# Two-layer decoder trunk on one core: sigmoid and head root moved ahead of four copies, one weighing moved ahead of the conv products, another between them, and fewer filler matmuls at the start

## The reference, cut to what matters

```python
mod = cond @ w_ada[l] + b_ada[l]                       # 1024 -> 6 * 1024
sh1, sc1, gt1, sh2, sc2, gt2 = split(mod, 6)
u = x * (1 + sc1) + sh1
q, k, v, o, i_pre, f_pre, cb, cc, ch = split(u @ w_in[l])
h = mlstm_chunkwise(q, k, v, i_pre, f_pre)             # 4 heads
h = head_norm(h, mh_norm_w[l]) * sigmoid(o)
y_conv = cb * depthwise_conv3(cc * ch)                 # 512 channels
mix = concat([h, y_conv]) @ w_out[l]
x = layer_norm(ALPHA * x + (1 + gt1) * mix)
u = x * (1 + sc2) + sh2
y = hier_moe(u)                                        # 16 experts, 1024 -> 512 -> 1024
x = layer_norm(ALPHA * x + (1 + gt2) * y)
```

## Time and profile before

| what | value |
|---|---|
| undisturbed runs | 839.2 and 839.71 us (a third run read 1674.44; 839.71 is the median of the three) |
| profiled execution: its time, its span | 841.6 us, 839.8 us |
| busy TensorE, VectorE, ScalarE, GpSimd | 94%, 46%, 12%, 9% of the span |
| mean granted clock of TensorE | 0.975 |
| mean traffic | 348 GB/s over the span, 292.54 MB |
| stages: head, mixer 0, routing, experts 0 | 0 to 28, to 184, to 204, to 430 us |
| mixer 1, routing, experts 1, last norm | to 588, to 604, to 828, to 840 us |

### The profile page before, as it was taken

How to read it: one execution, slowest core, us unless ns; L and a number is a source line. 1 busy time by engine, 2 the same in 40 slices (tenths; PEclk the granted TensorE clock), 3 DMA queues, 4 the chain that set the end, 5 groups by cost and what they waited for, 6 DMA issues and landing times.

```text
span 839.8 us, 9226 instructions
## 1 busy us (share of the span) xinstructions
PE 791.5 (94%) x3804; PEld 428.8 (51%) x3823; DVE 390.3 (46%) x818; ACT 98.9 (12%) x213; POOL 71.4 (9%) x94
## 2 busy tenths in 40 slices
PE   7999996989999999999979999699899999999994
PEld 2775685655444344434337658575544434443431
DVE  0138836997433313431346656393643431334135
ACT  2021101103111011101120200110311101110100
POOL 4000150120100000000002303003010000000000
PEclk9999997999999999999989999899999999999998
DMA  9993998797999999999996577487599999999991
GB/s 318 398 403 141 376 373 312 271 401 282 393 407 415 415 409 415 416 409 414 415 409 247 221 297 264 159 308 292 204 393 386 414 413 410 414 416 409 415 413 68
DMA packets 71029, 292.54 MB, mean 348 GB/s; under 512 B 4496, under 2 KB 4776, under 8 KB 62792
## 3 DMA queue, kind: packets, MB, share of 16 engines
q1 hardware_dynamic: 68712, 291.62, 87.9%
q0 software_dynamic: 1216, 0.25, 0.2%
q10 hardware_dynamic: 1056, 0.03, 0.1%
HBM read 290.84 MB, written 1.05 MB: 348 GB/s over the span
## 4 chain that ended last, share of the span: by engine, by line
PE 79%; DVE 9%; DMA 6%; issue 4%; ACT 1%; POOL 1%; DVEq 0%; POOLq 0%
PE bank L806 22%; PE bank L701 13%; PE bank L830 12%; PE bank L793 8%; PE bank L718 7%; DMA ring<-in_w_up_dram 6%; PE bank L852 4%; PE bank L965 2%; DVE bench L1246 2%; PE bank L732 2%; PE bank L577 2%; DVE expo L1246 1%; PE bank L591 1%; PE bank L814 1%; PE bank L860 1%
## 5 line engine op out<-in xcount | busy, mean ns | idle before, releaser
L701 PE MATMUL bank<-uT,ring 128*128 128x256 f32 x512 | 113.4, 381 | 0.0
L701 PEld LDWEIGHTS bank<-uT,ring 128*128 128x128 f32 x512 | 96.4, 190 | 17.0 <-issue 4.3
L830 PE MATMUL bank<-ring,hb 128*64 128x512 f32 x448 | 99.6, 595 | 1.4 <-ACT hb L1103 1.4
L806 PE MATMUL bank<-ring,uT 128*64 128x512 f32 x448 | 99.2, 593 | 1.0 <-DMA ring<-in_w_up_dram 1.0
L806 PE MATMUL bank<-ring,qT 128*64 128x512 f32 x448 | 99.4, 594 | 0.0
L1246 DVE SCALAR_TENSOR_TENSOR bench<-ring,cond,bench 128x1024 f32<-128x1024 f32 x63 | 82.7, 1314 | 4.7 <-DMA ring<-in_w_ada_dram 2.6
L793 PEld LDWEIGHTS bank<-ccT,X 128*128 128x128 f32 x512 | 61.5, 197 | 11.0 <-issue 11.0
L1469 DVE SCALAR_TENSOR_TENSOR kT<-bank,share,v_flat 128x512 f32<-128x512 f32 x32 | 23.9, 748 | 92.3 <-PE bank L830 92.3
L793 PE MATMUL bank<-ccT,X 128*128 128x128 f32 x512 | 64.3, 284 | 0.3 <-DVE ccT L1422 0.3
L806 PEld LDWEIGHTS bank<-ring,uT 128*64 128x64 f32 x448 | 31.6, 137 | 63.7 <-issue 60.5
L830 PEld LDWEIGHTS bank<-ring,hb 128*64 128x64 f32 x448 | 30.9, 137 | 62.8 <-issue 60.5
(11 more groups left out here) (284 smaller groups left out, 704.6 us busy)
## 6 DMA issues: line engine op xcount, KB each, us to landing
ring<-in_w_gate_dram SPq DMA_DIRECT2D x28, 2048.0 KB, 17.2
ring<-in_w_up_dram SPq DMA_DIRECT2D x28, 2048.0 KB, 17.7
ring<-in_w_down_dram SPq DMA_DIRECT2D x28, 2048.0 KB, 15.7
ring<-in_w_ada_dram SPq DMA_DIRECT2D x23, 2048.0 KB, 12.5
ring<-in_w_in_dram SPq DMA_DIRECT2D x14, 2048.0 KB, 16.0
ring<-in_w_out_dram SPq DMA_DIRECT2D x4, 2048.0 KB, 10.3
bench<-in_w_gate_dram SPq DMA_DIRECT2D x4, 2048.0 KB, 13.4
bench<-in_w_up_dram SPq DMA_DIRECT2D x4, 2048.0 KB, 17.3
```

Source lines behind the costliest of these rows:

```text
L701: last = pe.matmul(bank[4 + i // 2][:, i % 2 * SEQ:(i % 2 + 1) * SEQ], w[:, j, col:col + P], uT[:, 4 * k + j, :], start=(k == 0 and j == 0 ...
L806: last = pe.matmul(bank[bk][CAP * j:CAP * (j + 1), :], xg[b][:, 4 * h + k, CAP * j:CAP * (j + 1)], ring[s[h]][:, 4 * j + k, :], start=(h = ...
L830: last = pe.matmul(bank[6 + half][CAP * j:CAP * (j + 1), :], hhT[:, f, CAP * j:CAP * (j + 1)], ring[s[h]][:, 4 * j + 2 * i + half, :], sta ...
```

## The change

It has four parts.

- ScalarE, both layers: the sigmoid and the head root stand ahead of the four `ccT` copies.
- VectorE, both layers: `ada_weigh(l, 9)` stands ahead of the four products, not between the second and the third. In layer 0, two halves of `ada_weigh(1, 1)` stand behind the first and the second product, and no longer ahead of `first_norm`.
- The unit `("ada", 1, 1)` stands ahead of `("proj", 0, 6)` in the list of transfers, four places earlier.
- TensorE: eleven filler matmuls fewer in the head, and three more in each layer ahead of the transposes behind the output projection.

```diff
-               ("proj", 0, 5), ("ada", 0, 8), ("ada", 0, 9), ("proj", 0, 6), ("ada", 0, 10), ("ada", 0, 11), ("wout", 0, 0),
-               ("ada", 1, 1), ("ada", 1, 2), ("ada", 1, 3), ("wout", 0, 1)],
+               ("proj", 0, 5), ("ada", 0, 8), ("ada", 0, 9), ("ada", 1, 1), ("proj", 0, 6), ("ada", 0, 10), ("ada", 0, 11), ("wout", 0, 0),
+               ("ada", 1, 2), ("ada", 1, 3), ("wout", 0, 1)],
...
                 ada_unit(0)
                 stay_busy(3, 3)
                 head_columns(0)
-                stay_busy(6, 3)
+                stay_busy(4, 3)
                 ada_unit(1)
                 small_columns()
-                stay_busy(3, 3)
                 head_columns(1)
                 transpose_x()
-                stay_busy(8, 4)
+                stay_busy(2, 4)
                 pe.wait_ge(uT_act, 4)
...
+                stay_busy(3, 4)
                 transpose_half(0, [(x_ready, 2 * T * l + 1)] * 2, rows_of, by_half)
...
-                for q in range(CH):
-                    act.wait_ge(proj_done, NBLK * l + 14 + 2 * q)
-                    act.activation(ccT[:, q, :], bank[4 + q][:, 0:SEQ], ACT.Copy).then_inc(proj_act, 1)
                 act.wait_ge(proj_act, 16 * l + 12)
                 link(act.activation(o_sig[:, :, :], o_sig[:, :, :], ACT.Ln, bias=1.0))
                 act.activation(o_sig[:, :, :], o_sig[:, :, :], ACT.Exp, scale=-1.0).then_inc(sigmoid_ready, 1)
                 rsqrt(0, T * HEADS, hvar_ready, l + 1, hrs_ready)
+                for q in range(CH):
+                    act.wait_ge(proj_done, NBLK * l + 14 + 2 * q)
+                    act.activation(ccT[:, q, :], bank[4 + q][:, 0:SEQ], ACT.Copy).then_inc(proj_act, 1)
...
+                ada_weigh(l, 9)
                 for q in range(CH):
                     dve.wait_ge(proj_done, NBLK * l + 14 + 2 * q)
                     dve.wait_ge(proj_act, 16 * l + 13 + q)
                     dve.tensor_tensor(zT[:, q, 2:2 + SEQ], ccT[:, q, :], bank[4 + q][:, SEQ:2 * SEQ], ALU.mult).then_inc(proj_dve, 1)
-                    if q == 1:
-                        ada_weigh(l, 9)
+                    if l == 0 and q < 2:
+                        ada_weigh(1, 1, 2 * q, 2 * q + 2)
...
                 if l == 0:
-                    for i in range(1, 4):
+                    for i in range(2, 4):
                         ada_weigh(1, i)
```

## The result

The changed kernel took 812.29 us (median of four runs, 811.26 to 815.0) beside 839.46 for the kernel before: ratio 0.9685, 95% interval [0.9654, 0.9715]. The profiled execution of after took 811.93 us with a span of 810.2; that of before had a span of 839.8. The medians differ by 27.2 us, the two profiled spans by 29.6.

A forecast was written before the change was run, and what follows sets the result against it. TensorE, busy 94%, was taken as the bound, with gains in its waits and half-clock stretches. Layer 0 10.4 + layer 1 9.3 + tail 4.4 + head 2.1 = 26.2 us: 841.6 to 815.4 profiled, median 813.5, range 809.5 to 821.

The forecast's parts named there:

- The wait and the slow stretch: TensorE before the first block: 7.5 us wait goes in each layer, plus slow matmuls of 2.9 and 1.8 us.
- with it goes the stretch at half clock: Layer 0, 48 matmul records behind the wait return to full clock: 13.35 to 10.4, 2.9 us saved.
- VectorE's walk in layer 0: VectorE's new order from ready heads at 116.2 through the products, ending between 127.9 and 132, in time for TensorE.
- GpSimd's share: Layer 0: GpSimd's reductions running beside VectorE's weighing were allowed to add 1 to 4 us.
- The tail: End of layer 0's mixer: VectorE begins the norm earlier, last transposes 3.3 us behind the projection instead of 7.7; 4.4 us.
- The head: Kernel start: eleven fillers removed save 2.6 us, first products at half speed give back 0.5; 2.1 us net.
- 2.6 gross: Kernel start: the eleven removed fillers, at 0.21 to 0.27 us each, save 2.6 us before any clock loss.
- Rival 1: The weight transfer stream caps layer 0, time 822 us; chance 0.15 wholly or in part (816 to 823).
- My walk: Layer 0 transfers: twelve units from 129.5 end at 192.7, just before TensorE's first expert buffer release at 193.3.
- Rivals 2 and 4: Head clock stays low through first products, 816 us, chance 0.12; or far longer, 844 at 60 us, slower, chance 0.02.
- rival 2: Clock stays low under the head's first products, losing 2.9 us, not 0.5; 816 us, chance 0.12.

The follow-up runs named there:

- e12: The changed kernel run and profiled once more, nothing altered: 813.54 us, ratio 0.9672 to the kernel before.
- e1: The kernel before with only ScalarE's sigmoid and head root moved ahead of the four cc copies: 822.16 us, ratio 0.9781.
- e3: The kernel before with 34 filler matmuls inside TensorE's wait ahead of the first block, both layers: 841.78 us, ratio 0.9997.
- e4: The changed kernel with the early unit back in its old place, in the transfer list and on VectorE: 819.38 us, ratio 0.9757.
- e6: The changed kernel without the three fillers ahead of the transposes behind the output projection: 813.28 us, ratio 0.9649.
- e5: The changed kernel with the head's eleven fillers put back: 814.18 us, ratio 0.9656.
- e7: The changed kernel with the tenth unit's weighing back between the second and third product, both layers: 813.04 us, ratio 0.964.
- e11: The kernel before with ScalarE's order, VectorE's order and the early unit's move, but all fillers as before: 814.31 us, ratio 0.9687.
- e8: The kernel before, unchanged, profiled once more: 841.0 us (one run).
- e2: The changed kernel with ScalarE's order of before (copies first), the rest of the change kept: 843.18 us, ratio 1.0023.
- e9: The changed kernel with 32 matmuls left out of layer 0's mixer and two early units weighed with half their operations: 810.04 us, ratio 0.9624.
- e10: The changed kernel with 32 matmuls left out of layer 1's mixer: 808.36 us, ratio 0.9611.

## Why the prediction was right, point by point

The forecast was 813.5 us; 812.29 was measured, and 813.54 in e12. For the profiled execution I forecast 815.4 and got 811.93.

**The wait and the slow stretch, both layers (19.7 forecast).** Right in mechanism and size: 7.5 + 2.8 and 7.5 + 1.7 in the traces, 19.4 by e1 (14 to 23 by its interval). I put the wait down to ScalarE's place in its queue, and e1 moves that alone. The step "with it goes the stretch at half clock" holds in both kernels' rows; e3 shows a condition that I didn't state: in layer 0 the 2.8 us count only if VectorE comes to the norm sooner as well. ScalarE's order sees to that by itself, by 10.7 us in e1.

**VectorE's walk in layer 0.** Forecast: last product done between 127.9 and 132, in the times of before; it was 127.5, and after runs 3.9 us ahead of before there (97.81 for 101.68 at the start of cc/ch), so 131.4, near the end of the range. GpSimd's share: I allowed 1 to 4 us; four operations beside its reduction of 112.70 to 116.77 took 7.10 us, two beside the next 4.13, for 5.2 and 2.60 undisturbed, so 3.4 in all. That is most of the 4.3 us by which the group of 63 is longer (1383 ns for 1314). The Trainium skill ("GPSIMD Engine Reference", 1. Specifications) says that GpSimd shares its SBUF interfaces with VectorE and contends with instructions that have two SBUF inputs, as a weighing has; the trace agrees, by these 3.4 us.

**The tail (4.4 forecast).** 4.7 in the trace, 3.0 us for 7.7. By e4 the early unit's move is worth about 6 in the median; its profile has 4.2 of that in the tail (7.2 for 3.0). The rest is not placed. The three new fillers, which I put at no cost and no gain, keep the clock up there, for 0.8 us (e6).

**The head (2.1 forecast).** 2.2 between the two profiles, but both had a fall of the clock there. At full clock it is 1.7, in three profiles against three, and by medians 0.9 and 1.1 (e5 against e6 and e7), within the noise of each; e11 against e12 gives 0.8 with the tail's fillers in it. The term of "2.6 gross" left out the transfer: 0.69 us of wait take its place.

**Rival 1, the stream of transfers.** It did not bind. My walk had its end at 192.7 and the release at 193.3; they were near 188.7 and 188.71, 4.0 and 4.6 us sooner, since I counted the units from 129.5 with 2 us to start, and the queue had issued the first w_out unit at 126.04 already; the release was sooner by the head, which I had not counted there, by the fall near 74 and by small terms. The margin was as thin as forecast.

**Rivals 2 and 4, the clock in the head.** It was back at 27 as forecast; in e12 it never fell. The Trainium skill's rule on transposes ("TensorE: Matmul & The Clock Gate", Part 4: PE-mode transpose), which I weighed for rival 2, is borne out in part only: the 16 transposes of x took 3.27 us with the clock falling in one profile of before and 1.94 at 1.00 in the other (e8), with the same instructions around them.

**What I left out.** The profile of before carried 12 us of falls of the clock, of which 4.4 belong to the waits. One of the others, near 74, does not come in every execution of the same kernel (before has it and e8 not, e12 has it and after not), and I subtracted my sum from a profile that held it: 1.7 of the 3.5 us between 815.4 and 811.93. The rest are small terms that I had at nothing: 0.3 in the routing, 0.4 at the end, the overlap of records at the two waits, and 0.6 in the experts and projections, which is a difference of falls of the clock. By the medians, which average over the falls, 26.2 was forecast and 27.2 found. That it came so close is in part luck: by medians the head gave about 1 for 2.1 and the early unit some 6 for 4.4, and neither is known to better than a few microseconds.

## What to carry to other kernels

Before an engine is called busy elsewhere, look at what it was doing when its input had been ready for 20 us: here ScalarE, at 12% load, sat in a wait for a copy that nobody else could start, and the sigmoid behind it held two other engines. Two edits on one path are not two terms: filling the wait was worth nothing because VectorE's queue was equally late, while ScalarE's order moved both engines and kept the same microseconds, so a term is to be checked against the engine that is next in line. And a difference of a few microseconds between two profiles is read against a second profile of the same kernel first.

## What the runs showed of the hardware

- The granted clock also fell with TensorE 100% busy, at a cost of 1.7 us each time, in full rows of matmuls behind a few short ones (74 to 78 in before, 452 to 457 in after). Two executions of one kernel share some of the places and not others: 74, 186 and 432, then 184, 430 and 471 in the two profiles of before; 452, then 71, 416 and 566 in the two of after. Of the fourteen profiles six have a fall in the row near 74, and five in the same row of layer 1. The falls are likely part of the spread of 836 to 846 us between runs of before.
- Three matmuls of zeros (0.8 us) between the output projection and the transposes go with a clock that stays at 1.00 through them: without them it fell, though TensorE had no wait there (e6, e11); with them and no wait of over 0.3 us it didn't (after, e12, e2, e5, e7, e9, e10).
- Where TensorE stood still for 7.5 us the clock fell each time (four of four); with matmuls of zeros in that time it stayed at 1.00 (e3, both layers).
- Behind the experts of layer 0 TensorE's sequencer stops for 4.0 to 4.4 us in twelve of the fourteen profiles, before and after alike, and not at all in e3 and e9, whose programs hold more and fewer matmuls ahead of that point. It costs 1.6 us where neither profile has a fall of the clock (after beside e9). The place is right behind a branch around a block that isn't run. That the stop depends on where the code lies is a guess; no run varied that alone.
